# Unread products on TensorE in the first mixer rounds, before the second block's logits and in the second mixer norm

## What is computed

```python
h = rms_norm(x, norm1_g[l]) * (1.0 + sc1) + sh1
z = h @ w_in[l]
ya = gmlp_mixer(za, gmlp_ws[l], gmlp_bs[l])
yb = dsa_mixer(zq, zk, zv, zqi, zki, zwi, rel_bias[:, :DSA_HEADS])
yc = pool_mixer(zc, pool_w[l], pool_scale[l])
yd = swa_mixer(zdq, zdk, zdv, swa_sinks[l], rel_bias[:, DSA_HEADS:])
y = _rms(jnp.stack([ya, yb, yc, yd], axis=2)).reshape(bsz, seq, D_MIX) * mix_out_g[l]
x = x + g1 * (y @ w_out[l])
h = rms_norm(x, norm2_g[l]) * (1.0 + sc2) + sh2
x = x + g2 * conv_glu(h, ffn_w_up[l], ffn_conv_w[l], ffn_conv_b[l], ffn_w_down[l])
return rms_norm(x, final_g)
```

## Time and profile before

| | us |
|---|---|
| median of 3 runs | 1287.73 |
| lowest, highest | 1284.63, 1289.82 |
| profiled execution, its own time | 1285.75 |
| profiled execution, first to last instruction | 1283.7 |
| PE busy, share of the span | 1206.8, 94% |
| PE weight loads | 993.3, 77% |
| DVE | 718.8, 56% |
| POOL | 630.3, 49% |
| ACT | 577.2, 45% |
| mean granted TensorE clock | 0.987 |

### The profile page before, as it was taken

One profiled execution on the slowest core, in us unless ns is written; L12 is line 12 of the kernel. 1 busy time (PEld: TensorE's weight loads), 2 busy tenths in 40 slices (PEclk: granted clock), 3 DMA queues, 4 the chain that ended last, 5 costly groups with the idle time before them and its releaser, 6 DMA issues.

```text
span 1283.7 us, 17073 instructions
## 1 busy us (share of the span) xinstructions
PE 1206.8 (94%) x5708; PEld 993.3 (77%) x5708; DVE 718.8 (56%) x1405; ACT 577.2 (45%) x993; POOL 630.3 (49%) x317
## 2 busy tenths in 40 slices
PE   2898999987899899999999999989999999999997
PEld 1687778866788788888878887878788888888876
DVE  6943877888966898989984344353621112211224
ACT  4236656545852444224422666553444234422443
POOL 1135566783405255445545566325255445544554
PEclk9999999998999999999999999999999999999999
DMA  8457753451122122232224443424222222222223
GB/s 315 155 184 258 204 160 132 149 152 33 50 82 98 50 99 98 98 114 94 89 96 148 139 139 114 145 76 142 70 96 97 98 99 98 98 97 91 93 102 141
DMA packets 58568, 153.91 MB, mean 120 GB/s; under 512 B 6505, under 2 KB 20201, under 8 KB 58513
## 3 DMA queue, kind: packets, MB, share of 16 engines
q1 hardware_dynamic: 47472, 135.12, 31.3%
q10 hardware_dynamic: 11040, 18.09, 4.3%
HBM read 142.66 MB, written 10.52 MB: 119 GB/s over the span
## 4 chain that ended last, share of the span: by engine, by line
PE 40%; issue 24%; POOL 15%; DVE 11%; DMA 4%; ACT 4%; ACTq 1%; POOLq 0%; SPq 0%; DVEq 0%
PE ps L1858 10%; POOL w_lo L559 10%; PE ps L1859 9%; PE ps L1861 9%; DVE unread L1332 4%; POOL act_lo L712 3%; PE ps L2145 2%; POOL w_ada L598 1%; PE ps L1839 1%; PE ps L1840 1%; PE ps L1842 1%; PE ps L2124 1%; PE ps L2134 1%; DMA w_ada<-in_w_ada 1%; DVE h_lo L1290 1%
## 5 line engine op out<-in xcount | busy, mean ns | idle before, releaser
L559 POOL TENSOR_TENSOR w_lo<-w_raw,w_hi 128x1024 fp32r<-128x1024 f32 x148 | 356.5, 2409 | 435.9 <-ACT w_hi L724 435.9
L1858 PE MATMUL ps<-h_hi,w_hi 128*128 128x512 f32 x896 | 355.8, 397 | 4.5 <-POOL w_lo L565 4.5
L1859 PE MATMUL ps<-h_lo,w_hi 128*128 128x512 f32 x896 | 350.7, 391 | 0.0
L1861 PE MATMUL ps<-h_hi,w_lo 128*128 128x512 f32 x896 | 331.9, 391 | 0.0
L724 ACT ACTIVATE w_hi<-w_raw 128x1024 fp32r<-128x1024 f32 x148 | 156.8, 1059 | 334.0 <-PE ps L1861 327.4
L1858 PEld LDWEIGHTS ps<-h_hi,w_hi 128*128 128x128 f32 x896 | 169.2, 189 | 40.3 <-POOL w_lo L565 5.7
L1861 PEld LDWEIGHTS ps<-h_hi,w_lo 128*128 128x128 f32 x896 | 168.9, 188 | 36.1
L1859 PEld LDWEIGHTS ps<-h_lo,w_hi 128*128 128x128 f32 x896 | 169.4, 189 | 32.5
L1732 DVE SCALAR_TENSOR_TENSOR ps<-conv_in,conv_w,ps 128x512 f32<-128x512 f32 x44 | 33.2, 753 | 206.4 <-ACT ps L1133 206.4
L1858 PE MATMUL ps<-act_hi,w_hi 128*128 128x512 f32 x352 | 140.3, 399 | 5.0 <-POOL act_lo L712 2.6
L1861 PE MATMUL ps<-act_hi,w_lo 128*128 128x512 f32 x352 | 137.4, 390 | 0.0
(11 more groups left out here) (252 smaller groups left out, 1849.6 us busy)
## 6 DMA issues: line engine op xcount, KB each, us to landing
w_raw<-in_w SPq DMA_DIRECT2D x173, 512.0 KB, 3.2
w_ada<-in_w_ada SPq DMA_DIRECT2D x48, 512.0 KB, 4.1
x_sb<-in_x SPq DMA_DIRECT2D x4, 1024.0 KB, 9.8
q_st<-qk_dram SPq DMA_DIRECT2D x32, 128.0 KB, 4.1
out<-fin_o ACTq DMA_DIRECT2D x16, 256.0 KB, 2.1
qi_st<-qi_dram ACTq DMA_DIRECT2D x18, 128.0 KB, 4.3
qk_dram<-qk_hi ACTq DMA_DIRECT2D x4, 512.0 KB, 3.0
qk_dram<-qk_lo ACTq DMA_DIRECT2D x4, 512.0 KB, 3.9
```

The source lines that it names most:

```text
L559: pool.tensor_tensor(r(w_lo[:, slot]), w_raw[:, slot], w_hi[:, slot], ALU.subtract).then_inc(w_lo_ready, 1)
L1858: pe.matmul(ps[:, bank], r(hi_t[:, kk]), r(xh(kk)), start=(i == 0), stop=False)
L1859: pe.matmul(ps[:, bank], r(hi_t[:, kk]), r(xl(kk)), start=False, stop=False)
L1861: mm = pe.matmul(ps[:, bank], r(lo_t[:, kk]), r(xh(kk)), start=False, stop=last_k)
```

## The change

`turn_over` takes a bank, and is called at three more kinds of places: 12 products into bank 6 between `gate_turn(3)` and `swa_logits(1)`; 4 into bank 6 in each `swa_turn` of the blocks 0 to 3, behind the wait for `swa_probs` and ahead of that for `swa_exp` (the two waits change places); and 5 into bank 3 ahead of the tiles i = 0, 2 and 4 of the second half's mixer norm. No other engine's instructions change.

```diff
-            def turn_over(count):
+            def turn_over(count, bank=IDLE_BANK):
                 for _ in range(count):
-                    pe.matmul(ps[:, IDLE_BANK, 0:P], ident[:], ident[:], start=True, stop=True)
+                    pe.matmul(ps[:, bank, 0:P], ident[:], ident[:], start=True, stop=True)
...
             def swa_turn(b, j):
+                pe.wait_ge(swa_probs, 2 * b + j)
+                if b < 4:
+                    turn_over(4, 6)
                 pe.wait_ge(swa_exp, HEADS * b + 2 * j + 2)
-                pe.wait_ge(swa_probs, 2 * b + j)
...
                 gate_turn(b)
                 if b == 3:
+                    turn_over(12, 6)
                     swa_logits(1)
...
                         pe.wait_ge(dsa_out_ready, HB * (h + 1))
+                    if h == 1 and i in (0, 2, 4):
+                        turn_over(5, 3)
                     if h == 0:
```

## The result

| | median | runs | lowest to highest | profiled execution, span |
|---|---|---|---|---|
| before | 1286.78 us | 18 | 1283.18 to 1289.99 | 1285.75, 1283.7 |
| after | 1291.24 us | 18 | 1286.73 to 1295.48 | 1289.48, 1287.4 |

The ratio of after to before is 1.0034, with the 95% interval 1.0023 to 1.0044. So the change costs some 4.4 us. That is less than the 0.5% of the prediction, but the interval leaves out 1. The forecast of 1289.5 us had the sign right and was 1.7 us short. Its loss of 1.8 us was 2.7 us short, less than half of the real one: the median of three runs from which it was counted stood 0.95 us above the one measured here.

A forecast was written before the change was run, and what follows sets the result against it. PE, busy 94% of 1283.7 us, bounds the kernel; 0 + 2.4 + 0 - 1.3 + 1.7 + 0.2 = +3.0 us, or +1.7 without the fall before round 0, gave 1289.4 to 1290.7; forecast 1289.5 us, range 1285 to 1293.5.

The forecast's parts named there:

- the 0.5% of the prediction: Whole kernel: about 0.5%, 6.4 us, is what its measurement can tell from no change; within it was given 0.92.
- Its loss of 1.8 us: Whole kernel: forecast 1289.5 us against the before median of 1287.73 us, a loss of 1.8 us or 0.14%.
- the median of three runs: Before kernel: the 1287.73 us to which the prediction added its shifts.

The follow-up runs named there:

- the second kind alone: The 32 products of rounds 0 to 3 added to the before kernel without the twelve: ratio 1.0031; with only rounds 0 and 1's sixteen: 1.0025.
- the thin ones: The 32 products of rounds 0 to 3 alone, each with one column of result instead of 128, against before: 1299.91 us, ratio 1.0090.
- the wide ones: The 32 products of rounds 0 to 3 alone, each with 128 columns of result, against before: 1289.61 us, ratio 1.0031.
- the twelve alone: Only the twelve products ahead of the second block's logits added to the before kernel: 1287.82 us, ratio 0.9989 (0.9968 to 1.0009).

## What to carry to other kernels

Unread products held the clock in this kernel, but not at every place and not in every execution. Price each group by where it stands. In a wait for another engine that is longer than the group it costs nothing; behind a wait that PE passes late it costs its whole time, here 0.9 us for four and about twice that while the clock is low. Two groups that are free or cheap alone need not be so together: in the two traces with both, the rounds 0 and 1 took longer than with the second kind alone. Filling one pause makes TensorE reach the next wait sooner, and the fall may move there, onto work that others wait for; look for the next wait before you fill this one. And where the clock decides, one trace of before is one draw: take a second, and price a fall by its chance, not by whether it is in one profile.

## What the runs showed of the hardware that was not expected

- A product with one column of result takes nearly the time of one with 128 (eight records 1.00 against 1.11 us), but does not do for the clock what the wide one does. With the thin ones PE was busy for 14.85 of 15 us (323 to 338) at 0.50; with the wide ones it was busy for 14.03 of 16 us (322 to 338) at 0.89.
- The same program shows falls of the clock at different places in different executions, with 3.7 us of difference over the 86 us of the first mixers alone, nearly as much as the whole effect of the change. Of this 2.9 us come from how long one fall lasts: it starts at about 315 us in both, and ends at 318 in the one and at 326 in the other.
- Nearly the same pause can end either way: ahead of block 1's window logits PE was idle for 1.85 us in after and 1.81 us in the twelve alone, behind the same twelve products, and the logits then ran at 0.50 in the one (1.98 us) and at 1.00 in the other (1.13 us). In the second execution of after PE was idle for longer, 2.02 us, and they ran at full clock (1.14 us).
